# Convolution and SiLU of the DeltaNet group per channel tile inside the projection, z/a/b products from the modulated rows, gates inside the norm stage

## The reference

```python
def short_conv(x, w):            # 5 taps, one weight per channel and tap, zero padding at both ends
    return lax.conv_general_dilated(x, w[:, None, :], window_strides=(1,), padding=[(pad, pad)], ...,
                                    feature_group_count=ch)

def deltanet_group(qkv, z, ab, ...):
    def prep(qkv_, ab_):
        y = jax.nn.silu(short_conv(qkv_, conv_w))
        q, k, v = split(y, 3)                       # 256 channels each, 4 heads of 64
        q = l2norm(q) * DN_HEAD_DIM ** -0.5
        k = l2norm(k)
        log_g = -exp(a_log) * softplus(ab[..., 0] + dt_bias)      # two directions, 4 heads
        beta = sigmoid(ab[..., 1])
        ...
    # then the chunked delta rule in both directions, rms_norm and silu(z)
```

## Time and profile before

| | |
|---|---|
| median of 3 runs | 6359.9 us (6359.7 to 6363.38) |
| span of the profiled execution, its own time by the profile | 6355.5 us |
| TensorE busy | 5181.8 us (82%) |
| DVE busy | 2266.1 us (36%) |
| ACT busy | 1043.6 us (16%) |
| POOL busy | 887.3 us (14%) |
| mean granted TensorE clock | 0.848 of full speed |

### The profile page before, as it was taken

One profiled execution on the slowest core, in us unless ns is written; L12 is line 12 of the kernel. 1 busy time (PEld: TensorE's weight loads), 2 busy tenths in 40 slices (PEclk: granted clock), 3 DMA queues, 4 the chain that ended last, 5 costly groups with the idle time before them and its releaser, 6 DMA issues. The chain is left out here.

```text
span 6355.5 us, 61045 instructions
## 1 busy us (share of the span) xinstructions
PE 5181.8 (82%) x23236; PEld 3839.2 (60%) x23236; DVE 2266.1 (36%) x3499; ACT 1043.6 (16%) x2044; POOL 887.3 (14%) x537
## 2 busy tenths in 40 slices
PE   6699868893787786999995798778937777699997
PEld 4354445762777555888883365537527776277775
DVE  1222132206555424333333222232055554334333
ACT  1111201202111112111103111112121111211011
POOL 0100010000101003333320000110000110134441
PEclk9787967596888888999997788785868888899999
DMA  3011011000000010101100010100000000011111
GB/s 128 13 40 40 0 53 40 0 14 6 1 0 0 27 40 20 40 33 40 40 26 32 13 53 27 53 13 0 14 6 0 0 0 27 13 40 46 46 46 46
DMA packets 18120, 171.01 MB, mean 27 GB/s; under 512 B 2160, under 2 KB 2416, under 8 KB 4208
## 3 DMA queue, kind: packets, MB, share of 16 engines
q1 hardware_dynamic: 16304, 159.39, 6.8%
q10 hardware_dynamic: 1728, 10.38, 0.4%
HBM read 165.57 MB, written 4.19 MB: 27 GB/s over the span
## 5 line engine op out<-in xcount | busy, mean ns | idle before, releaser
L936 PE MATMUL ps<-temp_parts,ring_parts 128*128 128x512 f32 (+1 forms) x2560 | 730.3, 371 | 140.4 <-DVE Hn_parts L1666 126.1
L936 PE MATMUL ps<-Yn_parts,ring_parts 128*128 128x512 f32 (+1 forms) x3840 | 798.5, 369 | 12.4 <-issue 12.4
L936 PEld LDWEIGHTS ps<-Yn_parts,ring_parts 128*128 128x128 f32 x3840 | 666.1, 188 | 144.8 <-issue 25.8
L543 PE MATMUL ps<-ring,temp 128*128 128x512 f32 (+2 forms) x1280 | 533.1, 567 | 225.6 <-POOL temp L1768 135.8
L936 PEld LDWEIGHTS ps<-temp_parts,ring_parts 128*128 128x128 f32 x2560 | 464.5, 190 | 233.1 <-issue 154.6
L543 PEld LDWEIGHTS ps<-ring,temp 128*128 128x128 f32 x1280 | 257.6, 208 | 460.2 <-issue 287.5
L1650 DVE SCALAR_TENSOR_TENSOR X<-ps,mods,X 128x256 f32<-128x256 f32 (+1 forms) x360 | 250.9, 697 | 785.4 <-PE ps L936 555.8
L1860 POOL TENSOR_TENSOR ring_parts<-ring,consts 128x2048 fp32r<-128x2048 f32 x64 | 298.8, 4669 | 1560.4 <-DMA ring<-in_ff 1002.9
L936 PE MATMUL ps<-Hn_parts,ring_parts 128*128 128x512 f32 (+1 forms) x1280 | 472.6, 369 | 0.0
L1673 DVE TENSOR_TENSOR Yn<-Yn 128x256 f32<-128x256 f32 (+1 forms) x160 | 187.6, 1173 | 462.9 <-ACT Yn_parts L1255 462.7
L518 PE MATMUL ps<-silu_c_sb,ring 128*128 128x2 f32 x1536 | 305.4, 337 | 54.7 <-DVEq L1347 33.7
(11 more groups left out here) (264 smaller groups left out, 6736.8 us busy)
## 6 DMA issues: line engine op xcount, KB each, us to landing
ring<-in_weights SPq DMA_DIRECT2D x42, 2048.0 KB, 7.9
ring<-in_ff SPq DMA_DIRECT2D x64, 1024.0 KB, 4.8
X<-in_x ACTq DMA_DIRECT2D x1, 5120.0 KB, 27.1
out_x<-X SPq DMA_DIRECT2D x1, 4096.0 KB, 12.0
Hn<-in_levels ACTq DMA_DIRECT2D x2, 896.0 KB, 4.5
consts<-in_consts ACTq DMA_DIRECT2D x1, 1473.0 KB, 11.4
temp<-in_w_uq ACTq DMA_DIRECT2D x2, 384.0 KB, 3.6
temp<-in_w_ukv ACTq DMA_DIRECT2D x2, 256.0 KB, 4.4
```

The costliest lines, as they stand in the source:

```text
L543: m = pe.matmul(ps[:, bank + j, 0:w_], src[:, k, :], w[:, k, 0:w_], start=(k == 0), stop=(k == KT - 1), skip_group_check=True)
L936: m = pe.matmul(ps[:, bank, 0:hi - lo], w[a][:, k, j * P:(j + 1) * P], x[b][:, k, lo:hi], start=(k == 0 and part == 0), stop=(k == k_n - 1 ...
```

## The change

The convolution leaves its own stage. `dn_project` on DVE now does, for each channel tile j: copy its odd products out of PSUM, finish the silu of tile j − 1, wait until all three products of tile j are copied, and make the five taps of tile j. ACT copies its even products of tile j and then computes the tanh of tile j − 1, in two pieces and straight into `raw`, which the taps have finished reading; `cv_t` is gone. The tanh of the sixth tile stands between ACT's copies of the second and third z tile. The z products read `Hm` itself; POOL's staging and its semaphore are gone, and the loop over z tiles is written out. The gates move into the norm stage: on ACT behind the four squares, on DVE ahead of the reciprocals. One barrier of each layer is gone on all engines.

```diff
@@ sizes and buffers
-        d_hst = [cut(Yn, 2 * NTOK + s_ * DM, KT, P)[0] for s_ in range(2)]
-        cv_t, _ = cut(Hn, j1, PADDED - 4)
@@ TensorE, dn_project
-                arrived()
-                with ln.loop(NT // 2, [("tile_in", 2), ("z_sb", 2)]):
-                    for s_ in range(2):
-                        pe.wait_ge(sems["z_sb"], nth("z_sb", s_ - 1, 2))
-                        tile_products(d_hst[s_], [272], 4 + s_, 1 + s_, 2)
+                w = arrived()
+                for t in range(NT):
+                    if t >= 2:
+                        pe.wait_ge(sems["z_sb"], nth("z_sb", t - 1))
+                    for k in range(KT):
+                        m = pe.matmul(ps[:, 4 + t % 2, 0:272], Hm[:, k, t * P:(t + 1) * P], w[:, k, 0:272],
+                                      start=(k == 0), stop=(k == KT - 1))
+                    m.then_inc(sems["z_mm"], tally("z_mm"))
@@ ACT, dn_project
+                def squash(j):
+                    act.wait_ge(sems["c_y"], nth("c_y", j + 1))
+                    A(raw[:, j, 0:NCTX], cv_y[:, 0:NCTX], ACT.Tanh, scale=0.5)
+                    A(raw[:, j, NCTX:NTOK], cv_y[:, NCTX + 4:NTOK + 4], ACT.Tanh, scale=0.5).then_inc(sems["c_tanh"], tally("c_tanh"))
+
+                for j in range(6):
+                    for n_ in range(3 * j, 3 * j + 3):
+                        if n_ % 2 == 0:
+                            lo, hi = SEGMENTS[n_ % 3]
+                            act.wait_ge(sems["prod"], nth("prod", n_ + 1))
+                            off = 2 if lo < NCTX else 6
+                            A(raw[:, j, lo + off:hi + off], ps[:, n_ % 4, 0:hi - lo], ACT.Copy).then_inc(sems["evac_act"], tally("evac_act"))
+                    if j:
+                        squash(j - 1)
...
+                for t in range(NT):
+                    if t == 2:
+                        squash(5)
+                    act.wait_ge(sems["z_mm"], nth("z_mm", t + 1))
+                    A(d_z[:, t, :], ps[:, 4 + t % 2, 0:256], ACT.Copy)
+                    A(d_ab[:, t, :], ps[:, 4 + t % 2, 256:272], ACT.Copy).then_inc(sems["z_sb"], tally("z_sb"))
@@ ACT, dn_norm
                 for j in NORM_ORDER:
                     A(n_sq[:, j, :], raw[:, j, 0:NTOK], ACT.Square).then_inc(sems["d_sq"], tally("d_sq"))
+                dn_gates_()
                 act.wait_ge(sems["d_stage"], nth("d_stage", 1))
@@ DVE, dn_project
+                def silu(j):
+                    dve.wait_ge(sems["c_tanh"], nth("c_tanh", j + 1))
+                    STT(raw[:, j, 0:NCTX], raw[:, j, 0:NCTX], 1.0, cv_y[:, 0:NCTX], ALU.add, ALU.mult)
+                    link(STT(raw[:, j, NCTX:NTOK], raw[:, j, NCTX:NTOK], 1.0, cv_y[:, NCTX + 4:NTOK + 4], ALU.add, ALU.mult))
+
+                for j in range(6):
+                    for n_ in range(3 * j, 3 * j + 3):
+                        if n_ % 2:
...
+                    if j:
+                        silu(j - 1)
+                    dve.wait_ge(sems["evac_act"], nth("evac_act", (3 * j + 2) // 2 + 1))
+                    dve.wait_ge(sems["evac_dve"], nth("evac_dve", (3 * j + 3) // 2))
+                    for k in range(5):
+                        src = raw[:, j, k:k + width]
+                        w_ = taps[:, j, k:k + 1]
+                        m = TS(cv_y, src, w_, None, ALU.mult) if k == 0 else STT(cv_y, src, w_, cv_y, ALU.mult, ALU.add)
+                        link(m)
+                    dve.sem_inc(sems["c_y"], tally("c_y"))
+                silu(5)
@@ every engine, list of stages (here DVE)
                 dn_project()
                 ln.barrier()
                 dn_gates_()
-                dn_conv()
-                ln.barrier()
                 dn_norm()
```

More of the change, by code:

```diff
@@ L1166, in dn_project @@
             def dn_project():
[L1167 to L1171, removed]
-                ln.passed("prod", 18)
[L1173 to L1177, removed]
+                def squash(j):
[11 more added lines that the diff above has]
+                        squash(j - 1)
+                ln.passed("prod", 18)
+                for t in range(NT):
[4 more added lines that the diff above has]
+                    A(d_ab[:, t, :], ps[:, 4 + t % 2, 256:272], ACT.Copy).then_inc(sems["z_sb"], tally("z_sb"))
+                ln.passed("c_y", 6)
+                ln.passed("z_mm", NT)
             def dn_gates_():
@@ L1190, in dn_gates_ @@
                 ln.passed("dn_gates", 2)
[L1192 to L1195, removed]
             def dn_norm():
@@ L1308, in _ @@
                 act.dma_start(Hn[:, j0:j1], d["levels"]).then_inc(sems["masks_in"], 16)
-                dn_gates_()
-                dn_conv()
-                ln.barrier()
                 dn_norm()
@@ L1514, in dn_project @@
                     m = dve.memset(raw[:, :, lo:lo + (4 if lo == 2 + NCTX else 2)], 0.0)
[L1515 to L1519, removed]
+                taps = par["conv"].rearrange("p (j k) -> p j k", j=6)
+                width = PADDED - 4
+                def silu(j):
[5 more added lines that the diff above has]
+                        if n_ % 2:
+                            lo, hi = SEGMENTS[n_ % 3]
+                            dve.wait_ge(sems["prod"], nth("prod", n_ + 1))
+                            off = 2 if lo < NCTX else 6
+                            TS(raw[:, j, lo + off:hi + off], ps[:, n_ % 4, 0:hi - lo], 1.0, None, ALU.mult).then_inc(sems["evac_dve"], tally("evac_dve"))
+                    if j:
[9 more added lines that the diff above has]
+                silu(5)
                 ln.passed("prod", 18)
+                ln.passed("c_tanh", 6)
             def dn_gates_():
@@ L1538, in dn_gates_ @@
                 ln.passed("dn_gates2", 2)
[L1540 to L1554, removed]
             def dn_norm():
@@ L1795, in plain_prep @@
                     pool.wait_ge(sems["z_mm"], nth("z_mm", 1, 1))
[L1797 to L1802, removed]
             def ret_backward(count, first):
@@ L1888, in _ @@
                 attend(1, swa_stage(NT - 1, 2), False)
-                ln.barrier()
-                dn_stage()
                 ln.barrier()
```

## The result

| | before | after |
|---|---|---|
| median of 4 runs | 6360.82 us (6359.7 to 6363.38) | 6218.59 us (6217.44 to 6221.34) |
| span of the profiled execution | 6355.5 us | 6215.8 us |
| TensorE busy | 5181.8 us | 5197.7 us |
| DVE busy | 2266.1 us | 2267.5 us |
| mean granted TensorE clock | 0.848 | 0.853 |

The account below looks back on a forecast made before the run. Before the norm the kernel was taken as serial: TensorE paces the projection, DVE the convolution stage with TensorE idle. Replacing 78.90 and 79.42 us by 9.57 per layer saves 139.2, so 6359.9 becomes 6221 us, range 6212 to 6234.

Parts of the forecast that it names:

- The sum: Both layers' savings before the norm, 69.33 and 69.85 us, together 139.2: span 6216.3, time 6220.7.
- the distance from span to median: Whole run: the median lies 4.4 us above the profiled span, and this was left unchanged.
- The stretch: From level-mask issue to the norm's first reciprocal: 78.90 and 79.42 us per layer fall to 9.57.
- The gates: On ACT between squares and first root in the norm stage: 2.36 us per layer, bounds 0 and 4.08.
- the estimate by that rule, 136.4: Total saving if each ACT table switch adds the skill's drain, making the gates cost 1.38 us more per layer.
- The cover: In the projection, DVE's 13.4 us per channel tile hides under TensorE's 17.27, with 3.9 to spare.
- The z tail: Sixth tile's taps and tanh under the z products: ready at 1412.2, TensorE wants 1413.8, cover 1.6 us.
- Staging at nothing: Z products: POOL's copies were already hidden, so taking them away gives nothing; ten tiles stay at 36.83 us.
- A, DVE as the pace: Projection: taps slow beside a busy TensorE, which waits for copies; 6259 us at 1.5 times the step, chance 0.05.
- B, the clock: Projection: waits for copies bring TensorE's lower clock back; 6507 us if all of it, chance 0.02.
- C, table switches: ACT in the projection switches tables between copy and tanh, making the z products late; 6223 or 6228 us, chance 0.03.
- D, no overlap: A wait holds the taps back until the projection ends; time stays about 6359 us, chance 0.01.

Follow-up runs that it names:

- conv_own_stage: Changed kernel with the convolution (taps, tanh, silu) put back in a stage of its own behind the projection, gates kept in the norm stage: 6343.3 us.
- after_again: The changed kernel, unedited, run again on one chip beside the kernel with three early squares: 6215.22 us.
- taps_plus5: Changed kernel with all five taps of every channel tile made twice on DVE, same results: 6236.1 us.
- tanh6_first: Changed kernel with the sixth tile's tanh ahead of ACT's copy of the first z tile instead of the third: 6232.14 us.
- before_z_direct: Kernel before with one part of the change: z products read the modulated rows directly, POOL's staging gone: 6357.76 us, ratio 1.0002.
- gates_own_stage: Changed kernel with the gates back in a stage and barrier of their own between projection and norm: 6220.37 us.
- taps_plus2: Changed kernel with two taps of every channel tile made twice on DVE, same results: 6220.59 us.
- squares_early: Changed kernel with three of the four squares moved on ACT between its copies of z tiles four to six: 6213.78 us.
- squares_early_gates_late: Kernel with three early squares, plus the gates moved on ACT behind the norm's last copies and DVE's share around the last reciprocal: 6213.84 us.
- the two repeated kernels: Changed kernel and the one with three early squares, both unedited, run again beside each other on one chip: 6215.22 and 6212.1 us.

## Why the prediction was right

**The sum.** It forecast a span of 6216.3 and a time of 6221 us (6212 to 6234); measured were 6215.8 and 6218.59. That the convolution's work would lie beside the projection was its main step. conv_own_stage shows it: 123.3 of the 139.4 us are overlap, one barrier per layer included. The other 16.1 went with the old stage too, and the prediction did not price them apart: the gaps of the loop (5.9 and 6.4 us) and the gates ahead of the taps (1.9 per layer). It did not need to, since it took the stretch as a whole and added up what is left in it.

**What was luck.** The stretches come out alike in every trace of this kernel (9.48 in after and in after_again), what lies outside them does not. Between the two stretches after has 3123.1 us and after_again 3120.0; behind the second they have 1636.8 and 1641.3. That the span met the forecast within 0.5 us is therefore in part luck; within a few us it is not. The time is 2.1 below the forecast of 6220.7: 0.5 is the span, and 1.6 is the distance from span to median, which I had left at 4.4 and which is 2.8.

**The stretch.** Forecast 9.57, measured 9.48 in both layers. The gates were put at 2.36, with 0 and 4.08 as bounds; on ACT they run from 1441.96 to the next table load at 1444.31, 2.35. DVE's part is hidden as argued. ACT's table loads are one of 1.28 at 1442.73, where the activations of 1442.35 + 0.36 have ended, and one at 1444.31. The first activation behind a load starts 1.29 after the load's start. The drain of about 1380 ns that the Trainium skill gives (ScalarE: Activation LUTs, What ACT_TABLE_LOAD costs) does not show in after either; the estimate by that rule, 136.4, is 3 short of the measured 139.4.

**The cover.** I put DVE's step at 13.4 us against 17.27. By taps_plus5 it is an estimated 10.3, so the cover is about 7 us and not 3.9. I had added the wait for ACT's copy and tanh in full (2.25), and most of it lies beside DVE's own copies. Two more terms were too large, also in the safe direction. The taps take 7.25 (1314.80 + 6.33 − 1313.88) and not 7.91, and the silu up to the next tap takes 1332.63 − 1331.04 = 1.59 and not 2.12, since the gaps of 0.18 to 0.57 that stood ahead of each dependent DVE instruction are not there in written-out code. In the kernel before, the waits of the loop compare a semaphore with a register and the operands' places follow the loop's counter; in after both are constants. That one of these is the reason is argued, and the two were not tried apart. The tanh in two pieces starts the next ACT work 1.46 later, not 1.65.

**The z tail.** I took 12.9 us from the last copy to the third z copy's end, and 1.6 us of cover. The chain is 1399.68 to 1410.96 + 0.18, 11.46, shorter by 1.5: the silu takes 0.53 less, the taps 0.66, the tanh 0.19, and the rest is in the copies. TensorE wants z tile five at 1399.48 + 4 × 3.68 = 1414.2: the cover is 3.1 and not 1.6. That the place is real is shown by tanh6_first and taps_plus5, which make it decide. That it would cost one us for each us of lateness, as I wrote, is wrong by the clock: in the first layer 4.00 of waiting cost 5.7, and 6.08 cost 8.2. In after the chain was never late, so the step did not bear on the time.

**Staging at nothing.** Right, by before_z_direct.

**The rivals.** A, DVE as the pace: its premise, that taps slow down beside a busy TensorE, is refuted by 6.33 us in both cases, and even twice the taps only reach 17.63. B, the clock: the projection kept 0.98. Its mechanism exists, though, as the two experiments with a wait show; the Trainium skill's account of it (TensorE: Matmul & The Clock Gate, HAM oscillation — how this bites in real kernels) speaks of a loss that is paid again at each of many waits. In these two experiments there is one wait per layer, and each was paid for once: behind it the clock was back at 1.00 after 4 to 5 us (from 1414.00 in tanh6_first, 1426.00 in taps_plus5). C, table switches: two loads between projection and root, and none in the projection, so it did not happen. D, no overlap, is refuted by 57.34 us of DVE in the projection's window.

## What to carry to other kernels

A stage in which the pacing engine of its neighbours stands at 0.00 can be worth nearly its whole length (here 69 of 72 us) if its work can be cut to pieces that become ready one by one in the stage before. Compare the step of the piece with the step of the engine that covers it, and then look at the last piece apart, since only there the cover ends. Price what is left by the one engine that stays in the open, in its order, here ACT with squares, gates and root. When a wait does fall on TensorE, count more than its length: here waits of 4.0 and 6.1 us cost 1.7 to 2.5 us more, because the rows behind them ran at a lower clock for 4 to 5 us.

## What the runs showed of the hardware that was not expected

The scan behind the norm runs ten rounds per layer. Before, from the third on, each takes 58.0 us, with a clock of 0.88. In after the same 356 matmuls per round go mostly through a cycle of 58.2, 59.7 and 55.9 us, in both layers, with a 59.4 or a second 58.2 here and there where 55.9 would be due. The windows of one round of before and then two of after:

```profile
1618.42:1676.45 58.03, 46.18 (x356) 42.06 (x356) 32.17 (x70) 9.40 (x18) 5.79 (x8) 0.88 0.00 0
```

```profile
1549.77:1605.70 55.93, 44.25 (x356) 40.02 (x356) 32.04 (x71) 9.40 (x18) 5.78 (x8) 0.94 0.00 0
1663.93:1723.67 59.74, 49.18 (x356) 44.00 (x356) 32.12 (x71) 9.39 (x18) 5.78 (x9) 0.83 0.00 0
```

The rounds differ in TensorE's busy time, 44.25 against 49.18, and in the clock, 0.94 against 0.83, and in hardly anything else. The nine distances from round to round, taken at the round's first product on TensorE, add up to 525.8 in after and 524.1 before in the first layer, and to 525.0 and 524.0 in the second, so here it costs 2.6 us in all. before_z_direct, gates_own_stage and taps_plus5 keep 58.0 in both layers; tanh6_first, taps_plus2 and squares_early cycle in the first alone; conv_own_stage, squares_early_gates_late and the two repeated kernels cycle in both. None of them has an edit in the scan.

Summed over both layers, the distances are 1046.8 us in the trace of squares_early, which was one of its short runs, and 1053.7 in that of squares_early_gates_late, which was one of its long ones; before has 1048.1. So the rounds alone make up to 7 us of difference, while the way from the first reciprocal to the first round is 45.1 us in every kernel but the one with the late gates (45.8). What decides the pattern was not found. It is a reason not to read differences of a few us between such kernels from medians, and to compare stretches of the trace.
